# A four-layer transformer block and a three-branch mixer on one core: reciprocals and turned queries ahead of the coming weight tile in the latent mixer

## The reference

```python
def mla_mixer(x, w_dqkv, q_norm_g, w_uq, kv_norm_g, w_ukv, w_out, cos_m, sin_m):
    cq, ckv, k_rope = jnp.split(x @ w_dqkv, [Q_LORA, Q_LORA + KV_LORA], axis=-1)
    q = (rms_norm(cq, q_norm_g) @ w_uq).reshape(B, S, MLA_HEADS, MLA_NOPE + MLA_ROPE)
    q_nope, q_rope = q[..., :MLA_NOPE], apply_rope(q[..., MLA_NOPE:], cos_m, sin_m)
    kv = (rms_norm(ckv, kv_norm_g) @ w_ukv).reshape(B, S, MLA_HEADS, MLA_NOPE + MLA_V)
    k_nope, v = kv[..., :MLA_NOPE], kv[..., MLA_NOPE:]
    k_rope = apply_rope(k_rope[:, :, None, :], cos_m, sin_m)
    q = jnp.concatenate([q_nope, q_rope], axis=-1)
    k = jnp.concatenate([k_nope, jnp.broadcast_to(k_rope, (B, S, MLA_HEADS, MLA_ROPE))], axis=-1)
    o = causal_block_attention(q, k, v, (MLA_NOPE + MLA_ROPE) ** -0.5)
    return o.reshape(B, S, MLA_HEADS * MLA_V) @ w_out
```

## Time and profile before

| what | us |
|---|---|
| median of three runs | 2459.3 (2459.07 to 2460.08) |
| the profiled execution's own time | 2460.07 |
| its span, first to last instruction | 2458.3 |
| TensorE busy | 2401.9 (98%) |
| VectorE busy | 1910.8 (78%) |
| ScalarE busy | 1345.7 (55%) |
| GpSimd busy | 419.8 (17%) |
| mean granted TensorE clock | 0.996 |

### The profile page before, as it was taken

One profiled execution on the slowest core, in us unless ns is written; L12 is line 12 of the kernel. 1 busy time (PEld: TensorE's weight loads), 2 busy tenths in 40 slices (PEclk: granted clock), 3 DMA queues, 4 the chain that ended last, 5 costly groups with the idle time before them and its releaser, 6 DMA issues. The chain is left out here.

```text
span 2458.3 us, 32890 instructions
## 1 busy us (share of the span) xinstructions
PE 2401.9 (98%) x12987; PEld 2019.2 (82%) x12987; DVE 1910.8 (78%) x2424; ACT 1345.7 (55%) x1659; POOL 419.8 (17%) x463
## 2 busy tenths in 40 slices
PE   9999999999999999999989999999999998999999
PEld 7888878888888888888878888888778776998998
DVE  6787679889875798898758888887676777897554
ACT  5554555655664556555555565654554465444442
POOL 0002310000011100000330000002369502680000
PEclk9999999999999999999999999999999999999999
DMA  9555446556553455565425565555345552336553
GB/s 285 172 194 171 138 144 199 188 188 191 187 183 125 155 189 188 192 202 186 154 70 188 185 210 186 186 181 173 119 147 185 175 175 73 120 121 206 171 188 112
DMA packets 313946, 418.11 MB, mean 170 GB/s; under 512 B 18761, under 2 KB 271042, under 8 KB 313794
## 3 DMA queue, kind: packets, MB, share of 16 engines
q1 hardware_dynamic: 313794, 416.01, 52.0%
HBM read 414.92 MB, written 1.05 MB: 169 GB/s over the span
## 5 line engine op out<-in xcount | busy, mean ns | idle before, releaser
L536 DVE TENSOR_TENSOR wlo<-raw,whi 128x2048 fp32r<-128x2048 f32 (+1 forms) x367 | 853.5, 2336 | 146.2 <-ACT whi L529 145.4
L529 ACT ACTIVATE whi<-raw 128x2048 fp32r<-128x2048 f32 (+2 forms) x372 | 695.2, 1887 | 6.6 <-DMA raw<-in_ffn_w_dram 3.7
L699 PE MATMUL ps<-whi,xh 128*128 128x512 f32 (+2 forms) x1295 | 482.0, 372 | 7.2 <-DVE wlo L1658 2.2
L701 PE MATMUL ps<-whi,xl 128*128 128x512 f32 (+2 forms) x1295 | 475.1, 367 | 0.0
L700 PE MATMUL ps<-wlo,xh 128*128 128x512 f32 (+2 forms) x1295 | 474.6, 366 | 0.0
L699 PE MATMUL ps<-whi,oh 128*128 128x512 f32 x944 | 381.1, 404 | 0.6 <-DVE wlo L536 0.6
L701 PE MATMUL ps<-whi,ol 128*128 128x512 f32 x944 | 369.8, 392 | 0.0
L700 PE MATMUL ps<-wlo,oh 128*128 128x512 f32 x944 | 368.8, 391 | 0.0
L699 PEld LDWEIGHTS ps<-whi,xh 128*128 128x128 f32 x1295 | 244.1, 188 | 53.3 <-issue 11.3
L701 PEld LDWEIGHTS ps<-whi,xl 128*128 128x128 f32 x1295 | 244.1, 188 | 40.3
L700 PEld LDWEIGHTS ps<-wlo,xh 128*128 128x128 f32 x1295 | 244.3, 189 | 38.0
(11 more groups left out here) (412 smaller groups left out, 4208.0 us busy)
## 6 DMA issues: line engine op xcount, KB each, us to landing
raw<-in_ffn_w_dram SPq DMA_DIRECT2D x350, 512.0 KB, 4.9
raw<-in_ffn_w_dram SPq DMA_DIRECT2D x88, 1024.0 KB, 5.0
raw<-in_w_ff_dram SPq DMA_DIRECT2D x32, 1024.0 KB, 5.4
raw<-in_w_out_dram SPq DMA_DIRECT2D x20, 1024.0 KB, 4.9
raw<-in_w_in_dram SPq DMA_DIRECT2D x20, 1024.0 KB, 5.1
raw<-in_dsa_w_in_dram SPq DMA_DIRECT2D x32, 512.0 KB, 4.7
raw<-in_dsa_w_in_dram SPq DMA_DIRECT2D x12, 1024.0 KB, 5.1
raw<-in_fox_w_in_dram SPq DMA_DIRECT2D x16, 512.0 KB, 4.9
```

What stands on the lines that cost most here:

```text
L529: act.activation(hi(u)[:, 0:w], raw[:, (slot[u] + 1) % SLOTS, 0:w], ACT.Copy).then_inc(sem("hi_ready"), n)
L536: dve.tensor_tensor(lo(u)[:, 0:w], raw[:, (slot[u] + 1) % SLOTS, 0:w], hi(u)[:, 0:w].bitcast(F32), ALU.subtract).then_inc(sem("lo_ready"), n)
L699: pe.matmul(o, ah, bh, start=start, stop=False, skip_group_check=True)
L701: return pe.matmul(o, al, bh, start=False, stop=stop, skip_group_check=True)
```

## The change

In VectorE's list of the pair loop, `turned_qk` of the pair after next (`turns_at(st, i + 1)`) moves from the head of pass i + 1 to pass i, between the two reciprocals, and all three stand directly behind `turned_p(i)`, ahead of `split_lo` and `latent_values`. Pass 0 keeps its own `turned_qk(1)` at its head.

```diff
                     for i in range(NP if mla else 0):
-                        for n in turns_at(st, i):
-                            turned_qk(n)
                         if i == 0:
+                            turned_qk(1)
                             recip(0)
                             recip(1)
                             split_lo_half(dve, u + 4, 1)
...
                         turned_p(i)
+                        if i + 1 < NP:
+                            recip(2 * i + 2)
+                            for n in turns_at(st, i + 1):
+                                turned_qk(n)
+                            recip(2 * i + 3)
                         if i < NP - 2:
                             split_lo(dve, attn_ahead(st, i))
                         if i in (2, 4, 5):
                             latent_values(*((2, 2), (3, 1), (3, 2))[(2, 4, 5).index(i)])
-                        if i + 1 < NP:
-                            recip(2 * i + 2)
-                            recip(2 * i + 3)
                         low(i)
```

## The result

The changed kernel takes 2471.08 us, the median of five runs (2468.73 to 2474.84), against 2459.3 us (2457.65 to 2460.08, five runs) of the kernel before beside it: a ratio of 1.0042, 95% interval 1.0031 to 1.0053, or 8 to 13 us slower; the two medians by themselves lie 11.8 us apart. Forecast were 2468.6 us, between 2464.0 and 2471.7. The profiled execution of the change took 2469.73 us with a span of 2467.9 us, 9.6 us over the span before.

What follows compares the result with a forecast made beforehand. TensorE, busy for 2401.9 of 2458.3 us, was taken to bound the kernel. The terms 3.3 + 2.5 + 0.1 + 3.4 = +9.3 us on 2459.3 us gave 2468.6 us, range 2464.0 to 2471.7 us.

Steps and rivals of the forecast that it cites:

- The two stalls: Passes 4 and 5: TensorE waits for the values' copy, +3.3 us before the last key-value tile, +2.5 us before the residual.
- one stall only: Rival: pass 5's values' copy has unseen slack, so only pass 4 stalls; 2462.7 to 2464.4 us, chance 0.05.
- Passes 0 to 3: Early passes of the pair loop: gains mostly given back, +0.1 us, between a gain of 0.3 and a loss of 0.6 us.
- the gain stays: Rival: TensorE's waits of 0.73 and 1.12 us in passes 1 and 3 go; 2457.4 us, not slower, chance 0.05.
- the share of GpSimd: Passes 0 and 2: VectorE's weight tile is delayed by a GpSimd multiplication, 0.3 us each, the 0.6 us loss end.
- The clock: Behind both stalls TensorE's clock falls to half: 1.7 us each, +3.4 us, between 0 and 5.2; two falls 0.48.
- the clock falls once: Rival: both stalls come in passes 4 and 5, but only one clock fall; 7.6 us, 2466.9 us, chance 0.25.

Runs made afterwards that it cites:

- second own order: Kernel before with turned queries', values' copies and unit 9's low part reordered, turned_p between the masked-score fronts in passes 1, 3, 4; 2455.72 us, ratio 0.9981.

## Why the prediction was right

- **The two stalls** came as worked out, 3.27 us for 3.3 and 2.46 for 2.5, by the line that was reckoned: copy, reciprocal, tile, values' copy. That this line is the cause is shown by undoing one part at a time: the values' copy ahead of it removes the stalls, the tile ahead of it shortens them by 2.2 and 1.75 us, either moved part alone makes stalls there. The rival *one stall only* is out.
- **Passes 0 to 3** cost 0.59 us, by the table to the turning in pass 5, where +0.1 was taken and -0.3 to +0.6 allowed. The waits of 0.73 and 1.12 us went, as the rival *the gain stays* has it; but 0.27 and 0.96 us for GpSimd came, and 0.69, 0.20 and 0.37 us more at the values' copy (1.16) and the turned probabilities (1.32, 1.49): +0.64 in all.
- In that sum **the share of GpSimd was put on the wrong side**. The prediction let VectorE's tile start late, 0.3 us. It is the multiplication that is late, since the tile starts just ahead of it; GpSimd's timeline of the changed kernel in pass 2:

```profile
1252.37 2.45 POOL L964 TENSOR_TENSOR pr<-pr,rs 128x128 f32<-128x128 f32 x1
1254.78 0.61 POOL L965 TENSOR_TENSOR pr<-pr,rs 128x256 f32<-128x256 f32 x1
```

  The tile ran from 1252.16 for 2.40 us, only 0.11 us more than before, and a multiplication of 0.40 us that began 0.21 us behind it took 2.45. TensorE's wait of 0.96 us at 1255.53 is for the one after it. The Trainium skill's page SBUF — State Buffer (section "Who interferes with whom") has the shared ports as an exclusive lock, for which the issue order decides who blocks, and the trace agrees; the prediction had cited it with the order of the two reversed. The kernel before had shown this order too: the 2.71 us at 1283.14 above are a multiplication begun 0.05 us behind the start of a tile.
- **The clock** was the step that failed in number: two falls at 1.7 us were forecast, with a chance of 0.48, and one came, at 1.62 us. So the loop's own loss is 7.94 us, which is the rival *the clock falls once* (7.6 us, 0.25), and not the forecast's 9.3.
- That the median still lies above the forecast has a cause that the prediction did not have. The 2.38 us lost at the kernel's start belong to the execution, not to the change, and the execution profiled before lost none there. So it is in part luck that 2471.08 us lies within the range, 0.6 us under its end: a second fall that did not come (1.7 us) was made up by a loss that nothing in the forecast stands for. On the second of the experiments' chips the change costs 2469.29 - 2461.57 = 7.7 us, about the loop's 7.94; the kernel before takes 2.3 us more there than in the first runs, as it would if most of its executions lost the start too, but no trace of it there shows that. Of the 11.8 us between the medians, the loop and the start make 10.3; the rest is open, as runs without a trace don't show where they lost it. Their mean granted clock only says that it was there: 0.995 in the run with the shortest span (2466.9 us), 0.992 in that with the longest (2473.0).

## What to carry to other kernels

Before an instruction that waits for another engine is moved up an in-order list, look at what is then behind it and which engine waits for that: here a wait of 2.3 us on VectorE cost TensorE 3 us or nothing, by whether one copy of 0.4 us stood behind it or ahead. Put the copies that free a PSUM bank first, and fill the time before a wait with the long work that nobody needs yet. Where the gain is a microsecond or two, compare the stretch in the traces as well as the medians.

## What the runs showed of the hardware that was not expected

**The same idle does not bring the same clock.** In both profiled executions of the change the clock fell behind the stall of 3.03 us and stayed up behind that of 2.94 us, some 13 us later with the same eight turning matmuls ahead; with the turned queries alone, too, it fell behind the first only. With the reciprocals alone it fell behind the 2.41 us in front of the residual, the place where 2.94 us brought none. Waits of 1.33 and 1.49 us brought a fall in one profiled execution and none in others. Why is open.

**At the kernel's start the clock depends on the execution.** The work there is the same in all eleven profiled executions. Matmuls started from 10.2 to 13.6 us, the granted clock there and the start of the pair loop's first turning:

| executions | matmuls | clock | loop begins at, us |
|---|---|---|---|
| before, queries alone, second own order | 24 | 1.00 | 1222.7 to 1223.1 |
| the change twice and the six others | 9 to 15 | 0.52 to 0.72 | 1224.7 to 1225.3 |

A difference of some 2 us between two single executions of this kernel can be that alone.
